# RMS norms and head norms of a two-block model: sums in column groups, root and reciprocal with tokens on partitions, 1 / rms spread by products with diagonals

## What is computed

```
def rmsnorm(x, g):
    xf = x.astype(jnp.float32)
    y = xf * lax.rsqrt(jnp.mean(xf * xf, axis=-1, keepdims=True) + EPS)
    return (y * g.astype(jnp.float32)).astype(x.dtype)

def hgrn2_readout(o, g, norm_g):
    b, n = o.shape[0], o.shape[1]
    return rmsnorm(o, norm_g).reshape(b, n, HG_VAL) * jax.nn.silu(g.astype(jnp.float32))
```

## Time and profile before

| | us |
|---|---|
| median of 3 runs | 3315.85 |
| lowest, highest | 3314.59, 3319.35 |
| profiled execution | 3321.42 |
| its span in the trace | 3319.6 |
| PE busy (share of the span) | 2773.6 (84%) |
| DVE busy | 1773.4 (53%) |
| ACT busy | 1309.8 (39%) |
| mean granted TensorE clock, full = 1 | 0.91 |

### The profile page before, as it was taken

The page is one execution under the profiler, slowest core; times in us unless marked ns, Lnnn a source line. Parts: engine busy times, 40 slices in busy tenths (PEclk is TensorE's granted clock), DMA queues, the critical chain, the costliest instruction groups (busy, mean ns, idle before and its releaser), DMA issues. The chain is left out here.

```text
span 3319.6 us, 36522 instructions
## 1 busy us (share of the span) xinstructions
PE 2773.6 (84%) x13502; PEld 2103.2 (63%) x13502; DVE 1773.4 (53%) x2812; ACT 1309.8 (39%) x2034; POOL 234.8 (7%) x200
## 2 busy tenths in 40 slices
PE   3999867777999958977599959985799997977898
PEld 1766556556888837866433338863578786765686
DVE  2599767537999954356400035414555554157554
ACT  2223344335888843332211134412454443025543
POOL 1000034001101000023000000001000000020000
PEclk7999988888999978988699979997799999969999
DMA  5455400127996143210499954430144443400342
GB/s 220 178 215 216 178 1 1 51 84 268 412 411 266 52 158 127 81 48 1 163 352 412 406 188 178 186 124 5 51 177 190 161 186 125 182 1 1 150 184 78
DMA packets 94352, 536.70 MB, mean 162 GB/s; under 512 B 10849, under 2 KB 12257, under 8 KB 70625
## 3 DMA queue, kind: packets, MB, share of 16 engines
q1 hardware_dynamic: 87120, 508.41, 40.0%
q0 software_dynamic: 6768, 24.64, 2.1%
q10 hardware_dynamic: 288, 1.32, 0.1%
HBM read 599.87 MB, written 22.54 MB: 187 GB/s over the span
## 5 line engine op out<-in xcount | busy, mean ns | idle before, releaser
L1088 PE MATMUL ps<-w_hi,x_hi 128*128 128x512 f32 x1136 | 455.5, 401 | 14.1 <-DVE w_lo L2585 8.1
L1090 PE MATMUL ps<-w_hi,x_lo 128*128 128x512 f32 x1136 | 448.6, 395 | 0.0
L1089 PE MATMUL ps<-w_lo,x_hi 128*128 128x512 f32 x1136 | 448.1, 394 | 0.0
L1088 PEld LDWEIGHTS ps<-w_hi,x_hi 128*128 128x128 f32 x1136 | 217.3, 191 | 59.6 <-DVE w_lo L2585 8.5
L1088 PE MATMUL ps<-x_hi,w_hi 128*128 128x512 f32 (+1 forms) x512 | 203.9, 398 | 57.1 <-DVE x_lo L441 35.4
L1090 PEld LDWEIGHTS ps<-w_hi,x_lo 128*128 128x128 f32 x1136 | 216.7, 191 | 46.9
L1089 PEld LDWEIGHTS ps<-w_lo,x_hi 128*128 128x128 f32 x1136 | 217.5, 191 | 43.9
L1088 PE MATMUL ps<-w_hi,hidden_hi 128*128 128x512 f32 x536 | 210.8, 393 | 7.8 <-DVE hidden_lo L2752 6.0
L1090 PE MATMUL ps<-w_hi,hidden_lo 128*128 128x512 f32 x536 | 208.8, 390 | 0.0
L1089 PE MATMUL ps<-w_lo,hidden_hi 128*128 128x512 f32 x536 | 208.6, 389 | 0.0
L1089 PE MATMUL ps<-x_lo,w_hi 128*128 128x512 f32 (+1 forms) x512 | 196.8, 384 | 0.0
(11 more groups left out here) (615 smaller groups left out, 5791.8 us busy)
## 6 DMA issues: line engine op xcount, KB each, us to landing
weights_A<-in_moe_gate SPq DMA_DIRECT2D x132, 512.0 KB
weights_B<-in_moe_up SPq DMA_DIRECT2D x132, 512.0 KB
weights_A<-in_ffn_gu SPq DMA_DIRECT2D x24, 2048.0 KB, 7.4
weights_B<-in_ffn_gu SPq DMA_DIRECT2D x20, 2048.0 KB, 7.5
weights_C<-in_moe_down SPq DMA_DIRECT2D x66, 512.0 KB
weights_D<-in_moe_down SPq DMA_DIRECT2D x66, 512.0 KB
weights_C<-in_ffn_down SPq DMA_DIRECT2D x24, 1024.0 KB, 6.2
second_weights<-in_moe_gate SPq DMA_DIRECT2D x44, 512.0 KB
```

Source lines behind the costliest of these rows:

```text
L1088: nc.tensor.matmul(out, w_hi, x_hi, start=first, stop=False)
L1089: nc.tensor.matmul(out, w_hi, x_lo, start=False, stop=False)
L1090: return nc.tensor.matmul(out, w_lo, x_hi, start=False, stop=last)
```

## The change

In `rms_norm`, even chunks are squared by ACT and odd ones by DVE, into four buffers. The sums use weights of ones with 32 columns; chunk k goes to the 32 PSUM partitions of group k % 4, so that each group accumulates its own chunks. ACT copies these partial sums to SBUF; for each 128 tokens one product with two columns of ones adds the groups up and leaves the totals with tokens on partitions. Root and reciprocal are then on 128 x 8 values (or 128 x 4). DVE multiplies identity matrices by them, which gives one diagonal matrix for each 128 tokens; ones times the diagonal puts 1 / rms on all partitions again, in PSUM, from where the scaling reads it. In `head_norm_gate` the totals are made straight from the squares in the same way, four products for each pair, one root and one reciprocal for all pairs, then the diagonals of all pairs, and the spreading products for each pair.

```diff
--- before.py
+++ after.py
@@ -293,20 +293,25 @@
 
         nc, ps = self.nc, self.ps
         halves = [(c, slice(c * SEQ, (c + 1) * SEQ)) for c in range(tokens // SEQ)]
+        nt, groups = tokens // P, min(4, chunks)
+        rows = 32 * groups
         with ExitStack() as ctx:
-            sq = self.sb(ctx, "squares", [P, 2, tokens])
-            root = self.sb(ctx, "root", [P, tokens])
-            rstd = self.sb(ctx, "rstd", [P, tokens])
-            with stage(nc, "squared summed rooted inverted scaled shifted") as (block, s):
+            sq = self.sb(ctx, "squares", [P, groups, tokens])
+            parts = self.sb(ctx, "square_parts", [P, tokens])
+            rstd = self.sb(ctx, "rstd", [P, 2 * nt])
+            diag = self.sb(ctx, "rstd_diagonal", [P, nt, P])
+            with stage(nc, "act_squared dve_squared summed copied totals rooted inverted diag_made spread scaled shifted") as (block, s):
                 @block.scalar
                 def _(act):
-                    for k in range(chunks):
-                        if k >= 2:
-                            act.wait_ge(s["summed"], k - 1)
-                        nc.scalar.activation(sq[:, k % 2, :], src(k, slice(0, tokens)), ACT.Square).then_inc(s["squared"], 1)
+                    for k in range(0, chunks, 2):
+                        if k >= groups:
+                            act.wait_ge(s["summed"], k - groups + 1)
+                        nc.scalar.activation(sq[:, k % groups, :], src(k, slice(0, tokens)), ACT.Square).then_inc(s["act_squared"], 1)
                     act.wait_ge(s["summed"], chunks)
-                    nc.scalar.activation(root[:], ps[:, 0, 0:tokens], ACT.Sqrt, bias=self.eps[:, 0:1],
-                                         scale=1.0 / (chunks * P)).then_inc(s["rooted"], 1)
+                    nc.scalar.activation(parts[0:rows, :], ps[0:rows, 0, 0:tokens], ACT.Copy).then_inc(s["copied"], 1)
+                    act.wait_ge(s["totals"], 1)
+                    nc.scalar.activation(rstd[:], ps[:, 1, 0:2 * nt], ACT.Sqrt, bias=self.eps[:, 0:1],
+                                         scale=1.0 / (32 * chunks * P)).then_inc(s["rooted"], 1)
                     if shift is not None:
                         for k in range(chunks):
                             act.wait_ge(s["scaled"], (k + 1) * len(halves))
@@ -317,18 +322,37 @@
                 @block.tensor
                 def _(pe):
                     for k in range(chunks):
-                        pe.wait_ge(s["squared"], k + 1)
-                        nc.tensor.matmul(ps[:, 0, 0:tokens], self.c("ones"), sq[:, k % 2, :],
-                                         start=(k == 0), stop=(k == chunks - 1)).then_inc(s["summed"], 1)
+                        j = k % groups
+                        pe.wait_ge(s["dve_squared" if k % 2 else "act_squared"], k // 2 + 1)
+                        nc.tensor.matmul(ps[32 * j:32 * j + 32, 0, 0:tokens], self.c("ones", 32), sq[:, j, :],
+                                         start=(k < groups), stop=(k >= chunks - groups)).then_inc(s["summed"], 1)
+                    pe.wait_ge(s["copied"], 1)
+                    for t in range(nt):
+                        last = nc.tensor.matmul(ps[:, 1, 2 * t:2 * t + 2], parts[0:rows, t * P:(t + 1) * P], self.c("ones", 2, p=rows),
+                                                start=True, stop=True)
+                    last.then_inc(s["totals"], 1)
+                    pe.wait_ge(s["diag_made"], 1)
+                    for t in range(nt):
+                        last = nc.tensor.matmul(ps[:, 2, t * P:(t + 1) * P], self.c("ones"), diag[:, t, :], start=True, stop=True)
+                    last.then_inc(s["spread"], 1)
 
                 @block.vector
                 def _(dve):
+                    for k in range(1, chunks, 2):
+                        if k >= groups:
+                            dve.wait_ge(s["summed"], k - groups + 1)
+                        x = src(k, slice(0, tokens))
+                        nc.vector.tensor_tensor(sq[:, k % groups, :], x, x, ALU.mult).then_inc(s["dve_squared"], 1)
                     dve.wait_ge(s["rooted"], 1)
-                    nc.vector.reciprocal(rstd[:], root[:]).then_inc(s["inverted"], 1)
+                    nc.vector.reciprocal(rstd[:], rstd[:]).then_inc(s["inverted"], 1)
                     dve.wait_ge(s["inverted"], 1)
+                    one = rstd[:].rearrange("p (t n) -> p t n", n=2)[:, :, 0:1]
+                    nc.vector.tensor_tensor(diag[:], self.c("ident").unsqueeze(1).to_broadcast([P, nt, P]),
+                                            one.to_broadcast([P, nt, P]), ALU.mult).then_inc(s["diag_made"], 1)
+                    dve.wait_ge(s["spread"], 1)
                     for k in range(chunks):
                         for c, t in halves:
-                            a, r, o = src(k, t), rstd[:, t], dst(k, t)
+                            a, r, o = src(k, t), ps[:, 2, t], dst(k, t)
                             if permuted and c == 0:
                                 a = a.rearrange("p (r w) -> p w r", w=64)
                                 r = r.rearrange("p (r w) -> p w r", w=64)
@@ -2387,32 +2411,43 @@
 
         nc, ps = self.nc, self.ps
         with ExitStack() as ctx:
-            sq = self.sb(ctx, "head_squares", [P, pairs, 2, SEQ])
-            root = self.sb(ctx, "head_root", [P, pairs, 2, SEQ])
-            with stage(nc, "squared summed rooted inverted scaled gated") as (block, s):
+            sq = self.sb(ctx, "head_squares", [P, pairs, 2 * SEQ])
+            diag = self.sb(ctx, "head_rstd_diagonal", [P, pairs, 4, P])
+            rstd = self.sb(ctx, "head_rstd", [P, 4 * pairs, 2])
+            with stage(nc, "squared totals rooted inverted diag_made spread scaled gated") as (block, s):
                 @block.scalar
                 def _(act):
                     for j in range(pairs):
-                        nc.scalar.activation(sq[:, j, :, :], O(j), ACT.Square).then_inc(s["squared"], 1)
-                    for j in range(pairs):
-                        act.wait_ge(s["summed"], j + 1)
-                        nc.scalar.activation(root[:, j, :, :], ps[:, j, :].rearrange("p (h t) -> p h t", h=2), ACT.Sqrt,
-                                             bias=self.eps[:, 0:1], scale=1.0 / P).then_inc(s["rooted"], 1)
+                        nc.scalar.activation(sq[:, j, :].rearrange("p (h t) -> p h t", h=2), O(j), ACT.Square).then_inc(s["squared"], 1)
+                    act.wait_ge(s["totals"], 1)
+                    nc.scalar.activation(rstd[:].rearrange("p i n -> p (i n)"), ps[:, 7, 0:8 * pairs], ACT.Sqrt,
+                                         bias=self.eps[:, 0:1], scale=1.0 / P).then_inc(s["rooted"], 1)
 
                 @block.tensor
                 def _(pe):
                     for j in range(pairs):
                         pe.wait_ge(s["squared"], j + 1)
-                        nc.tensor.matmul(ps[:, j, :], self.c("ones"), sq[:, j, :, :].rearrange("p h t -> p (h t)"),
-                                         start=True, stop=True).then_inc(s["summed"], 1)
+                        for i in range(4):
+                            last = nc.tensor.matmul(ps[:, 7, 8 * j + 2 * i:8 * j + 2 * i + 2], sq[:, j, i * P:(i + 1) * P], self.c("ones", 2),
+                                                    start=True, stop=True)
+                    last.then_inc(s["totals"], 1)
+                    for j in range(pairs):
+                        pe.wait_ge(s["diag_made"], j + 1)
+                        for i in range(4):
+                            last = nc.tensor.matmul(ps[:, j, i * P:(i + 1) * P], self.c("ones"), diag[:, j, i, :], start=True, stop=True)
+                        last.then_inc(s["spread"], 1)
 
                 @block.vector
                 def _(dve):
+                    dve.wait_ge(s["rooted"], 1)
+                    nc.vector.reciprocal(rstd[:], rstd[:]).then_inc(s["inverted"], 1)
+                    dve.wait_ge(s["inverted"], 1)
                     for j in range(pairs):
-                        dve.wait_ge(s["rooted"], j + 1)
-                        nc.vector.reciprocal(root[:, j, :, :], root[:, j, :, :]).then_inc(s["inverted"], 1)
-                        dve.wait_ge(s["inverted"], j + 1)
-                        nc.vector.scalar_tensor_tensor(out=O(j), in0=O(j), scalar=scale, in1=root[:, j, :, :],
+                        nc.vector.tensor_tensor(diag[:, j], self.c("ident").unsqueeze(1).to_broadcast([P, 4, P]),
+                                                rstd[:, 4 * j:4 * j + 4, 0:1].to_broadcast([P, 4, P]), ALU.mult).then_inc(s["diag_made"], 1)
+                    for j in range(pairs):
+                        dve.wait_ge(s["spread"], j + 1)
+                        nc.vector.scalar_tensor_tensor(out=O(j), in0=O(j), scalar=scale, in1=ps[:, j, :].rearrange("p (h t) -> p h t", h=2),
```

## The result

The changed kernel took 3293.22 us (median of 4 runs, 3292.93 to 3297.10) against 3316.74 for the kernel before (4 runs, 3314.59 to 3319.35): ratio 0.9931, 95% interval 0.9914 to 0.9949, so 23.5 us faster. The forecast was 27. Run again, with runs of the kernel before on the same chip beside it, it took 3296.54 against 3314.20, ratio 0.9943 (0.9926 to 0.9959), 17.7 us. The profiled execution's span fell from 3319.6 to 3291.6, by 28.0.

What follows compares the result with a forecast made beforehand. The prediction took each norm's whole chain, ending in a barrier, as the bound, not DMA. Savings of 18.7 + 8.0 + 2.6 - 2.1 made 27 us, from 3315.85 to 3289 us; range 3276 to 3304.

Steps and rivals of the forecast that it cites:

- the rivals with another sign or without the groups' overlap: Small products cost more than they save, 3321 us, chance 0.04; column groups do not run side by side, 3309, 0.04.
- head 1: The head norm with 4 pairs: 15.4 us forecast against 23.41 before, 8.0 saved.
- N1 to N5: Four norms on 512 tokens and a fifth on 256: together 18.7 us saved.
- The walk: Step-by-step timing of squares and sums, 512 tokens: last product ends at 6.35 us at half clock, 4.25 at full.
- The ladder: Copy, totals, root, reciprocal, diagonals and spreading behind the sums, 512 tokens: 4.3 us at full clock, 6.2 at half.
- half clock for the sums and full behind them: PE's clock assumed in the first, second and fourth 512-token norms: 6.35 + 4.3 = 10.65 us each.
- The first rival: PE stays at half clock behind the sums: 13 us saved, 3303 us, chance 0.14.
- the prediction's own signs of being wrong: Summing 8 us or more, root over 1.4 behind copy, totals and spreading at clock 0.50, PSUM scaling clearly over 0.48.
- 32 instructions of totals, 12 of them at 0.24 and 20 at 0.13: Totals in the 4-pair head norm, clock rising on the way: done at 6.3 us.
- Head 2: The head norm with 2 pairs: 10.6 us forecast against 13.16 before, 2.6 saved.
- cq, ckv: Norms of 2 chunks and 1 chunk, 256 tokens: about 5.6 and 5.4 us, 0.7 and 1.4 lost.
- the rival made of rows: Table load holds up the root in three norms, 1.4 us each, 4.2 of the gain: 3293 us, chance 0.04.

Runs made afterwards that it cites:

- wide totals: Changed kernel with the totals' products, in norms and heads, moving 128 columns of ones instead of 2: 3297.05 us, ratio 0.9947.
- the gate ahead: Changed kernel with DVE multiplying by scale and gate in the heads while PE makes the totals, ahead of the spreading: 3291.21 us, ratio 0.9932.
- filled gaps: Changed kernel with idle PE products in the gaps of rms_norm: 3292.75 us; with more beside the scaling: 3291.15 us.
- the two last versions: Changed kernel with wide totals, the gate ahead, cq and ckv as before: 3286.49 us; the same plus idle products in 512-token norms' gaps: 3281.30 us.
- the last but one: Changed kernel with wide totals, the gate ahead, cq and ckv as before, without idle products: 3286.49 us, ratio 0.9921.

## Why the prediction was right, point by point

**The sum of 27 us.** Measured 23.5, and 17.7 in the repeat; both times are in the range, and the direction with a chance of 0.92 was right; the narrower span of "20 to 34 us saved" holds for the first and not for the second. The profiles have the gain in the stages named, 25.8 and 22.9 us of it in the nine norms, and the rivals with another sign or without the groups' overlap fell. The forecast still stood 3.5 to 9 too high, and the profiles say in which terms. Two of its sums are off by their own terms: head 1 adds up to 15.1 and not 15.4, and the gain of N1 to N5 at full clock to 26.0 and not 25.7. Neither changes the outcome.

**The sums.** The walk gave 6.35 at half clock and 4.25 at full. From first square to copy N2 took 6.0, N1 5.3 (part of it at full clock), N3 4.3. Right within 0.4 at half clock, and the groups of 32 columns run beside each other as those of 2 and 16 did: one group costs 3.5 us more in N3.

**The ladder.** 4.3 at full clock forecast; N3 took 4.2 (700.09 to 704.30). At half clock 6.2 forecast; N2 took 5.95 (588.44 to 594.39). Each step was within about 0.1 us of its term but for the totals at half clock, 1.9 against 2.1. The scaling from PSUM cost nothing.

**The clock behind the sums, N1, N2, N4.** This was named as the choice with the most weight, and "half clock for the sums and full behind them" was right for no norm in full: the two profiles of the changed kernel show 10.62 and 11.97, 11.97 and 10.87, 10.92 and 11.10 against 10.65 forecast. On average 0.6 too little each. That N1's 10.62 meets the 10.65 is luck: the clock rose within its sums, 4.4 us after the first square, which made them 5.3 instead of 6.35, and was down again for the spreading, which made the ladder 5.3 instead of 4.3. The first rival, the half clock stays, was true of one norm in each profile, and with it one of the prediction's own signs of being wrong: in N2, and in N1 in the repeat, totals and spreading ran at 0.50, and N2's root stood 1.95 behind the copy. What held it up was the totals, which end 0.03 before it, and not the load, which ends 0.66 before it.

**Head 1, the step that failed.** "32 instructions of totals, 12 of them at 0.24 and 20 at 0.13" took the rise of the clock from products with 512 columns. With two columns it did not come: 32 at 0.22. Head 1 lasted 16.9 and 17.5 against 15.4. The run with wide totals shows this to be the cause in head 1: 15.07 there, the clock up 4.4 us after the first square. "The spreading hidden beneath at full clock" was half right: DVE waited 0.37 once, and the run with the gate ahead shows how little was left beneath. Head 2: 10.92 against 10.6, with the exposed first spreading at 2.1.

**N5, cq, ckv.** 5.45 and 6.81 against the mean of 6.6 between both clocks. cq 4.89 and 5.33 against 5.6, ckv 5.29 against 5.4: ckv longer, as said; cq equal in the first profile and 0.45 longer in the second, so its 0.7 was too much.

**The table load.** Neither the drain of the Trainium skill (ScalarE: Activation LUTs, "What ACT_TABLE_LOAD costs") nor the rival made of rows came: in N1 the root follows the load of 1.28 by 0.02 us, in N2 the load ends 0.66 before it, under the totals.

**What follows each norm.** It moved up as a whole but for a few us. From N3 to N4 it is 496.1 to 496.6 us in the profiles with the changed N3 (494.4 to 495.5 with filled gaps or in the two last versions) where the old N3 has 493.8 to 493.9. Two of these us are in one wait at the end of the experts, from the list of waits of the kernel after:

```profile
POOL tile_rows L1276 <- DMA y_slots<-tile_out: 69.4, 1, 69.4
```

It is 67.4 in the kernel before, in the one with the old norms and in the three with filled gaps, 68.8 in the last but one, and 69.4 to 69.8 in all others. Up to there no instruction of DVE stands more than 0.4 us off its place in the kernel before, counted from N3's first scaling, in either profile of the changed kernel. Why a store some 460 us behind the norm lands 2 us later with one form of it and not with another is open; no run was made for it.

## What to carry to other kernels

Where every stage ends in a barrier, a norm's chain can be priced step by step from rows of the same program, and terms of 0.2 to 2 us add up to within a few us; what does not add up is the clock of TensorE, so each such step wants a price at either level, and more than one profile. Summing over partitions in column groups gave most of the norms' gain here; moving root and reciprocal to tokens on partitions was about even for 512 tokens, and a loss for one chunk of 256 at half clock. In the heads, where each pair had a long reciprocal of its own, it gave 6 to 8 us. A step taken off the last engine of a chain (the gate, off DVE) pays in full only once the engine before it is quick enough: alone it gave 0.4 to 1.1 us in head 1, with wide totals 2.5.

## What the runs showed of the hardware that was not expected

32 f32 instructions of products with two moving columns kept PE busy for 7.0 us at a granted clock of 0.50 throughout; with 128 moving columns and the same weights they took 5.6 us, the clock rose on the way, and what stood behind them ran at 1.00. This holds for head 1; in head 2 one of three profiles with wide totals stayed at 0.50. At half clock the narrow products save little: eight instructions with two columns took 1.87 us in N2, eight with 128 columns 2.08.

A busy PE is no sign of full clock: in an unedited stage behind N1 PE was busy for 13.6 us without a pause at 0.50 in one profile, and for 6.8 in another, with the same code there.

The same kernel on the same inputs had N1 at 0.66 and N2 at 0.50 in one profile and the reverse in another, 1.1 to 1.4 us of difference in each; one profile of such a stage is not its price.
